# Sixteen value copies for thirty-two, pairs in groups of queries, and probability turns as two turns of 64 rows

## The chip, the cores and the metric

One core of a Trainium2 chip. The metric is device microseconds of one execution, median of three runs: 2372.79 us (2370.24 to 2383.06).

## The reference

A sequence of 512 tokens of width 1024, float32, goes through two layers of a first block and one layer of a second. A layer of the first block is

```
x = x + 0.5 * swiglu(rms_norm(x), ...)            # ffn 1, hidden width 2816
p = rms_norm(x) @ w_in                            # four groups of 256
y = concat(na(p_a), mla(p_b), diff(p_c), gqa(p_d))
x = x + y @ w_out
x = x + 0.5 * swiglu(rms_norm(x), ...)            # ffn 2
x = rms_norm(x)
```

The neighbourhood mixer (na) lays the 512 tokens out as 8 rows of 64 columns. The columns are cut into four blocks of 16; the queries of a block see keys and values of a window of 32 columns in all 8 rows, with a learned bias per relative place and a mask. So a block has 128 queries and 256 keys. The other three mixers are full attention over 512 keys: mla with latents, diff with the difference of two maps and a T5 bias, gqa with two query heads per key head. Each has four heads.

The second block's layer projects x once more and mixes it with forgetting attention (fox, causal, four heads), stick-breaking attention, an RWKV recurrence and a gated linear recurrence.

## The kernel before

All weights are split in a high and a low part and multiplied three times. The feed-forward stages keep TensorE full. The order of work is written out by hand: each engine has one program, and semaphores tie them.

Around the change there are two places.

The attention stage of a layer (lines 1346 to 1443 for TensorE, 2182 to 2228 for ScalarE, 3138 to 3180 for VectorE) works through 40 pairs. A pair (`PAIRS`, line 153) is a mixer, a tile of 128 queries (for na: a block) and two heads or maps. In step s TensorE makes the scores of pair s (line 1391), then turns the probabilities of pair s - 2 (line 1404: blocks of 128x128 against the identity, from SBUF to two PSUM banks), then multiplies the turned probabilities of pair s - 3 with the values (`weigh`, line 1343: two halves of 64 queries on column groups), then does what else is set for the step (turns of queries, keys and mixed values at line 1301; the two latent products at 1311 and 1313). VectorE adds the bias and finds the maxima (3079; 3073 without a bias), makes the difference of the two maps for diff (3064), and takes the mixed values out with the reciprocal of the sum (3104, 3091). ScalarE makes the exponentials (2209) and copies the turned probabilities from PSUM to SBUF (2201; 2199 for diff). For na and diff a turn has four blocks (diff turns only the difference, in one bank), for gqa and mla eight. Scores of na and gqa contract over 64 rows, one head on rows 0 to 63 and the other on 64 to 127, of diff over 32, of mla over 96.

The values of na need another layout than the projection has: for each of the four blocks the 256 tokens of its window, on partitions. `spread_values` (line 970), in SP's queue, makes it with DMAs from SBUF to SBUF: for each token tile t, as soon as ScalarE has copied it out of PSUM with its scale (line 2093, semaphore `proj_copied`), for each block and each of the tile's two grid rows one DMA of 32 tokens by 256 values, 32 in all. All count on one semaphore, `na_v_loaded`; TensorE waits for all 32 ahead of the first product of na. `na_v[0]` holds blocks 0 and 1, `na_v[1]` blocks 2 and 3. The pairs of na are ordered by heads first: blocks 0 to 3 with heads 0 and 1, then blocks 0 to 3 with heads 2 and 3.

The second place is `fox` (line 1560, ScalarE's part at 2402): 8 units of two heads and one query tile, with one to four key tiles each, in the same manner of steps. Its turns stand at line 1589 (with eight blocks at most) and its copies at 2410.

Of the kernel before, what the change touches and what calls it, by code (L numbers as in the profile page):

```python
# [14 lines left out]
P = 128  # L15
# [133 lines left out]
NA_ROOM = 4 * 7 * P  # L149
assert NA_KH == NA_ROWS and NA_B == T and len(NA_FORMS) * HEADS * NA_KEYS <= NA_ROOM  # L150


def attention_pairs():
# [3 lines left out]
    na, mla = ([(m, i, (h, h + 1)) for h in (0, 2) for i in tiles] for m in ("na", "mla"))  # L157
# [189 lines left out]
def build_program(nc, A, out):  # L347
    ctx = ExitStack()
    with ctx:
# [172 lines left out]

        SCORE, TURNED, MIXED, MISC = 0, 2, 4, 6
# [105 lines left out]
        na_v_loaded = sem("na_v_loaded")  # L629
# [129 lines left out]
        small_loaded = sem("small_loaded")  # L759
# [143 lines left out]
        def _(sp):  # L903
# [94 lines left out]
            for n, pieces in enumerate(IN2_PANELS):  # L998
                if n == 2:

                    sp.wait_ge(x_ready, at_layer(DEPTH - 1, 4, 3))
                    sp.dma_start(cols2[:, :], A["cols2"]).then_inc(small_loaded, 16)
                    sp.dma_start(na_flat[:, 0:N_SMALL_CONST], A["small"]).then_inc(small_loaded, 16)
                    sp.dma_start(small("ln_g"), A["rwkv_ln_g_2"][0].partition_broadcast(P)).then_inc(small_loaded, 16)
                    sp.dma_start(small("ln_b"), A["rwkv_ln_b_2"][0].partition_broadcast(P)).then_inc(small_loaded, 16)
                    sp.dma_start(small("lora_w")[0:RW_LORA], A["rwkv_w2_2"][0]).then_inc(small_loaded, 16)
                    sp.dma_start(small("lora_w")[RW_LORA:2 * RW_LORA], A["rwkv_a2_2"][0]).then_inc(small_loaded, 16)
                    for name, w in (("w_a", "lru_w_a_2"), ("w_x", "lru_w_x_2")):
                        for par in range(2):
                            sp.dma_start(small(name)[par * HD:(par + 1) * HD].rearrange("i (h j) -> i h j", h=2),  # L1010
                                         A[w][0, par::2].rearrange("h i j -> i h j")).then_inc(small_loaded, 16)
# [32 lines left out]
        def _(pe):  # L1044
            def turn_x(c):
                pe.wait_ge(x_loaded[c], 16 if c else 16 * 3)
                for k in range(c * KB, (c + 1) * KB):
                    for t in range(T):
                        last = pe.transpose(bank[k][:, t * P:(t + 1) * P], x_tok[:, t, k * P:(k + 1) * P], ident[:, :])
                    last.then_inc(x_turned, 1)  # L1050

# [294 lines left out]
            def attention(l):  # L1346
# [20 lines left out]
                for step in range(N_STEPS):  # L1367
# [25 lines left out]
                    if 0 <= p < N_P:  # L1393
# [71 lines left out]
            def project2():  # L1465
                for m, (n, kind, at, t) in enumerate(IN2_STEPS):
                    if t == 0:
                        split(DEPTH, n)
                    if m == PE_BESIDE["gates"][0]:
                        pe.wait_ge(small_loaded, 16 * 10)  # L1470
# [89 lines left out]
            def fox():  # L1560
                pe.wait_ge(in2_tok, len(IN2_TOK))
                pe.wait_ge(in2_feat, len(IN2_FEAT))
                for step in range(N_FOX + 3):
# [19 lines left out]
                    if 0 <= u < N_FOX:  # L1583
# [3 lines left out]
                        for j in range(2):  # L1587
                            for t in range(FOX_UNITS[u][1] + 1):
                                last = pe.transpose(bank[4 + j][:, t * P:(t + 1) * P],
# [2225 lines left out]
```

## Time and profile before

| | |
|---|---|
| median of 3 runs | 2372.79 us |
| profiled execution | 2371.9 us, span 2370.1 us |
| TensorE matmul busy | 2318.9 us (98%) |
| VectorE busy | 1618.8 us (68%) |
| ScalarE busy | 1144.0 us (48%) |
| mean granted TensorE clock | 0.995 |
| first attention stage | about 475 to 624 us of the span |
| second attention stage | about 1472 to 1620 us |
| fox | about 2186 to 2214 us |

The span is from the first to the last instruction of the profiled execution; the time around it is 1.8 us. Busy shares are averages over stages with different limits, so a stage is read by itself. In the profile PE is TensorE's matmul row, PEld its weight loads, DVE is VectorE, ACT is ScalarE, SP the queue that issues the loads. L1343 is line 1343 of the kernel. A matmul's duration holds its latency, so matmuls of one row overlap.

### The profile page before, as it was taken

Reading aid. Unit: us, or ns where it says so; the run is one execution under the profiler, and the core shown is the slowest. Engines: PE = TensorE matmul, PEld = TensorE weight load, DVE = VectorE, ACT = ScalarE, POOL = GpSimd, SP = SyncE. Lnnn points to the kernel's source line nnn. Section 1 sums busy time; section 2 is a strip of 40 time slices with the busy share of each in tenths; the row PEclk is TensorE's granted clock in tenths of the full one; section 3 lists DMA queues with packets and bytes.
Section 4 is the critical chain, followed back from the end, with each engine's and each line's share of the span. In section 5 each row is a group of like instructions: output and inputs, shape, how many; then the busy total and the mean of one; then the engine's idle time right before and its main releaser. Section 6 shows DMA issues by size and latency. Waiting matters only on the chain.

```text
span 2370.1 us, 40655 instructions
## 1 busy us (share of the span) xinstructions
PE 2318.9 (98%) x16692; PEld 1989.6 (84%) x16692; DVE 1618.8 (68%) x2547; ACT 1144.0 (48%) x1949; POOL 24.0 (1%) x20
## 2 busy tenths in 40 slices
PE   8999999989999999999999999999999999999998
PEld 6999998846789999989999887567899998779687
DVE  7957665558679577689577654686786686682564
ACT  4535444467445354545344445674453455343623
POOL 0000001000000000000000010000000000000000
PEclk9999999999999999999999999999999999999999
DMA  5323342200233334333334422003333333222001
GB/s 155 107 90 102 113 158 91 87 14 18 72 89 100 97 94 115 95 93 104 94 98 117 165 83 80 22 1 90 89 99 98 104 106 118 84 85 72 1 10 65
DMA packets 276649, 205.89 MB, mean 87 GB/s; under 512 B 10673, under 2 KB 263569, under 8 KB 275953
## 3 DMA queue, kind: packets, MB, share of 16 engines
q1 hardware_dynamic: 275632, 195.96, 27.9%
q0 software_dynamic: 832, 7.33, 0.8%
q8 instruction: 133, 2.18, 0.4%
q14 instruction: 52, 0.42, 0.1%
HBM read 199.06 MB, written 2.10 MB: 85 GB/s over the span
## 4 chain that ended last, share of the span: by engine, by line
PE 87%; DVE 6%; ACT 3%; DVEq 2%; issue 1%; DMA 0%; ACTq 0%; SPq 0%
PE bank L1082 23%; PE bank L1174 10%; PE bank L1176 10%; PE bank L1175 10%; PE bank L1151 6%; PE bank L1152 6%; PE bank L1153 6%; PE bank L1360 4%; PE bank L1391 2%; PE bank L1343 2%; PE bank L1454 2%; PE bank L1404 2%; PE bank L1699 1%; PE bank L1301 1%; DVE h_lo L2682 1%
## 5 line engine op out<-in xcount | busy, mean ns | idle before, releaser
L2533 DVE TENSOR_TENSOR w_lo<-raw,w_hi 128x2048 fp32r<-128x2048 f32 (+2 forms) x117 | 240.4, 2055 | 160.0 <-ACT w_hi L1886 159.8
L1886 ACT CAST w_hi<-raw 128x2048 fp32r<-128x2048 f32 (+2 forms) x118 | 202.3, 1715 | 182.3 <-PE bank L1153 90.2
L1151 PE MATMUL bank<-hid_hi,w_hi 128*128 128x512 f32 x704 | 274.7, 390 | 0.9 <-DVE xT L2774 0.9
L1152 PE MATMUL bank<-hid_lo,w_hi 128*128 128x512 f32 x704 | 274.3, 390 | 0.0
L1153 PE MATMUL bank<-hid_hi,w_lo 128*128 128x512 f32 x704 | 273.9, 389 | 0.0
L1174 PE MATMUL bank<-h_hi,w_hi 128*128 128x256 f32 x864 | 245.0, 284 | 2.0 <-DVE w_lo L2718 1.5
L1176 PE MATMUL bank<-h_hi,w_lo 128*128 128x256 f32 x864 | 244.5, 283 | 0.0
L1175 PE MATMUL bank<-h_lo,w_hi 128*128 128x256 f32 x864 | 244.5, 283 | 0.0
L2718 DVE TENSOR_TENSOR w_lo<-raw,w_hi 128x1024 fp32r<-128x1024 f32 x144 | 175.4, 1218 | 3.2 <-ACT w_hi L1958 3.2
L1174 PEld LDWEIGHTS bank<-h_hi,w_hi 128*128 128x128 f32 x864 | 165.7, 192 | 3.9 <-issue 1.6
L1175 PEld LDWEIGHTS bank<-h_lo,w_hi 128*128 128x128 f32 x864 | 165.7, 192 | 0.9
L1176 PEld LDWEIGHTS bank<-h_hi,w_lo 128*128 128x128 f32 x864 | 165.7, 192 | 0.0
L1082 PE MATMUL bank<-h_hi,w_hi 128*128 128x512 f32 x416 | 163.9, 394 | 0.2 <-DVE w_lo L3261 0.2
L1176 PE MATMUL bank<-ops_hi,more_lo 128*128 128x256 f32 x576 | 163.0, 283 | 0.0
L1174 PE MATMUL bank<-ops_hi,more_hi 128*128 128x256 f32 x576 | 162.9, 283 | 0.0
L1082 PE MATMUL bank<-h_lo,w_hi 128*128 128x512 f32 x416 | 162.0, 389 | 0.0
L1082 PE MATMUL bank<-h_hi,w_lo 128*128 128x512 f32 x416 | 161.9, 389 | 0.0
L1082 PE MATMUL bank<-w_hi,h_hi 128*128 128x512 f32 (+2 forms) x448 | 159.8, 357 | 0.0
L1082 PE MATMUL bank<-w_hi,h_lo 128*128 128x512 f32 (+2 forms) x448 | 158.4, 353 | 0.0
L1082 PE MATMUL bank<-w_lo,h_hi 128*128 128x512 f32 (+2 forms) x448 | 158.3, 353 | 0.0
L1151 PEld LDWEIGHTS bank<-hid_hi,w_hi 128*128 128x128 f32 x704 | 132.3, 188 | 28.9 <-issue 2.5
L1153 PEld LDWEIGHTS bank<-hid_hi,w_lo 128*128 128x128 f32 x704 | 132.2, 188 | 27.8
(501 smaller groups left out, 5459.5 us busy)
## 6 DMA issues: line engine op xcount, KB each, us to landing
raw<-in_ffn_w_up SPq DMA_DIRECT2D x88, 512.0 KB, 5.3
raw<-in_ffn_w_gate SPq DMA_DIRECT2D x87, 512.0 KB, 4.0
raw<-in_ffn_w_down SPq DMA_DIRECT2D x96, 384.0 KB, 3.7
raw<-in_w_in SPq DMA_DIRECT2D x60, 512.0 KB, 4.6
raw<-in_w_out SPq DMA_DIRECT2D x24, 512.0 KB, 4.5
raw<-in_ffn_w_down SPq DMA_DIRECT2D x16, 512.0 KB, 4.4
t_bias<-in_t_rel POOLq DMA_DIRECT2D x2, 1792.0 KB, 10.8
raw<-in_w_in SPq DMA_DIRECT2D x8, 416.0 KB, 3.8
```

The lines of the kernel that those rows point to most:

```text
L1082: last = pe.matmul(to, left[a](k), right[b](k), start=(begin and k == 0 and a + b == 0), stop=(end and k == n - 1 and a == 1))
L1151: pe.matmul(to, hi(k), hid_hi[:, k, :], start=(k == 0), stop=False)
L1152: pe.matmul(to, hi(k), hid_lo[:, k, :], start=False, stop=False)
L1153: last = pe.matmul(to, lo(k), hid_hi[:, k, :], start=False, stop=(k == n - 1))
L1174: pe.matmul(columns_at(to), w_hi_[:, k, :], x_hi[:, k, :], start=(begin and k == 0), stop=False, skip_group_check=True)
L1175: pe.matmul(columns_at(to), w_hi_[:, k, :], x_lo[:, k, :], start=False, stop=False, skip_group_check=True)
L1176: last = pe.matmul(columns_at(to), w_lo_[:, k, :], x_hi[:, k, :], start=False, stop=(k == HALF_K - 1), skip_group_check=True)
L1343: last = pe.matmul(to[half * HD:(half + 1) * HD], share[:, half * HD:(half + 1) * HD], value, start=begin, stop=end)
L1360: last = pe.matmul(bank[d % 4], w[:, k, cut], h[:, k, :], start=(begin and k == ks[0] and w is hi and h is h_hi), stop=(end and k == ks[-1 ...
L1886: act.copy(w_hi[:, at, 0:n], raw[:, at, 0:n]).then_inc(hi_ready[at], 1)
L2533: dve.tensor_tensor(w_lo[:, at, 0:n], raw[:, at, 0:n], w_hi[:, at, 0:n].bitcast(F32), ALU.subtract)\
L2718: dve.tensor_tensor(w_lo[:, at, cut], raw[:, at, cut], w_hi[:, at, cut].bitcast(F32), ALU.subtract)\
```

## The change

Values: SP makes 16 DMAs, each of 32 partitions by two token tiles. A copy in the list `NA_COPIES` is a half (token tiles 0 and 1, or 2 and 3) and a block. The half chooses the 64 partitions on which the values go, the grid row the 32 of them. So the keys of a block stand in another order, and the score side follows: ScalarE writes the turned keys of token tile t to place `NA_TILE[t]`, and the host lays the bias out by `NA_KEY_ROWS`. There are two semaphores, one for `na_v[0]` and one for `na_v[1]`; the pairs of na are ordered by blocks first, and TensorE waits for each semaphore ahead of the first product that reads its values. To have a semaphore free, the ten loads of small constants count on `const_loaded` (16 * 12 with the two loads before it) and `small_loaded` goes.

Turns: every turn of probabilities, in the attention stages and in fox, goes through `turn_halves`: each 128x128 block is turned as two turns of 64 rows, rows 0 to 63 into bank b and rows 64 to 127 into bank b + 1, each with 64 columns of result. ScalarE's copy reads the two banks by turns (`from_halves`) and leaves the same turned probabilities as before, in fox packed without gaps.

```
+NA_TILE = [t // 2 + t % 2 * 2 for t in range(T)]
+NA_KEY_ROWS = [2 * NA_TILE.index(n) + r for n in range(T) for r in range(P // GRID_W)]
+NA_COPIES = [(0, 0), (0, 1), (0, 2), (1, 0), (1, 1), (0, 3), (1, 2), (1, 3)]
+N_NA_COPIES = len(NA_COPIES) // 2 * (P // GRID_W)
...
-    na, mla = ([(m, i, (h, h + 1)) for h in (0, 2) for i in tiles] for m in ("na", "mla"))
+    na = [("na", i, (h, h + 1)) for i in tiles for h in (0, 2)]
+    mla = [("mla", i, (h, h + 1)) for h in (0, 2) for i in tiles]
...
+        def from_halves(b, n):
+            return two_banks(b)[:, :, 0:n * HD].rearrange("p h (n q) -> p n h q", n=n)
...
             def spread_values(l):
-                for t in range(T):
-                    sp.wait_ge(proj_copied, at_layer(l, N_COPY, N_COPY - T + t + 1))
-                    for b, a in enumerate(NA_AT):
-                        for r in range(P // GRID_W):
-                            kt, to = divmod((t * (P // GRID_W) + r) * NA_W, P)
-                            sp.dma_start(na_v[b // 2][to:to + NA_W, b % 2 * len(NA_KT) + kt, :],
-                                         proj[r * GRID_W + a:r * GRID_W + a + NA_W, t, NA_V:NA_V + G]).then_inc(na_v_loaded, 16)
+                for half, b in NA_COPIES:
+                    sp.wait_ge(proj_copied, at_layer(l, N_COPY, N_COPY - T + 2 * half + 2))
+                    for r in range(P // GRID_W):
+                        to, a = half * HD + r * NA_W, r * GRID_W + NA_AT[b]
+                        sp.dma_start(na_v[b // 2][to:to + NA_W, b % 2 * len(NA_KT):(b % 2 + 1) * len(NA_KT), :],
+                                     proj[a:a + NA_W, 2 * half:2 * half + 2, NA_V:NA_V + G]).then_inc(na_v_loaded[b // 2], 16)
...
+            def turn_halves(b, parts):
+                for n, part in enumerate(parts):
+                    for half in range(2):
+                        rows_ = slice(half * HD, (half + 1) * HD)
+                        last = pe.transpose(bank[b + half][:, n * HD:(n + 1) * HD], part[rows_], ident[rows_, rows_])
+                return last
...
-                        for j in (1,) if single else (0, 1):
-                            for t in range(key_tiles(p)):
-                                last = pe.transpose(bank[PAIR_TURNED + j][:, t * P:(t + 1) * P],
-                                                    pair_probs(p)[:, j, t * P:(t + 1) * P], ident[:, :])
-                        last.then_inc(probs_turned, 1)
+                        turn_halves(PAIR_TURNED, [pair_probs(p)[:, j, t * P:(t + 1) * P] for j in ((1,) if single else (0, 1))
+                                                  for t in range(key_tiles(p))]).then_inc(probs_turned, 1)
...
-                        if p == FIRST["na"]:
-                            pe.wait_ge(na_v_loaded, at_layer(l, 16 * S // NA_W * NA_B // 2, 16 * S // NA_W * NA_B // 2))
+                        if PAIRS[p][0] == "na" and PAIRS[p][1] % 2 == 0 and PAIRS[p][2][0] == 0:
+                            pe.wait_ge(na_v_loaded[PAIRS[p][1] // 2], at_layer(l, 16 * N_NA_COPIES, 16 * N_NA_COPIES))
...
-                        if PAIRS[p][0] == "diff":
-                            last = act.copy(to, bank[PAIR_TURNED + 1])
-                        else:
-                            last = act.copy(to.rearrange("p (j s) -> p j s", j=2), two_banks(PAIR_TURNED)[:, :, 0:n * P])
+                        to = turned_probs(p)
+                        n = to.shape[1] // P
+                        last = act.copy(to.rearrange("p (n h q) -> p n h q", n=n, h=2), from_halves(PAIR_TURNED, n))
```

Fox's turn and copy are changed in the same way, with `turn_halves(4, ...)` and `from_halves(4, 2 * n // P)`.

## Rows read from the trace of the kernel before

**Rows 1.** The page, the chain that ended last, by engine.

```profile
PE 87%; DVE 6%; ACT 3%; DVEq 2%; issue 1%; DMA 0%; ACTq 0%; SPq 0%
```

**Rows 2.** Timeline of PE, 478 to 516 us: start, length, line, tiles, count [idle before].

```profile
480.14 0.66 PE L1404 MATMUL bank<-ident,spare_hi 128*128 128x128 f32 x4
488.17 1.12 PE L1343 MATMUL bank<-na_v,probsT 128*64 128x64 f32 x16 [7.38 <-issue]
...
492.25 1.12 PE L1343 MATMUL bank<-na_v,spare_lo 128*64 128x64 f32 x16
...
495.01 0.69 PE L1343 MATMUL bank<-na_v,probsT 128*64 128x64 f32 x16
...
497.32 0.69 PE L1343 MATMUL bank<-na_v,spare_lo 128*64 128x64 f32 x16
...
502.32 1.13 PE L1391 MATMUL bank<-work 32*128 32x512 f32 x4
503.38 0.66 PE L1404 MATMUL bank<-ident,probs 128*128 128x128 f32 x4
...
514.19 1.10 PE L1404 MATMUL bank<-ident,probs 128*128 128x128 f32 x8
515.22 0.69 PE L1343 MATMUL bank<-wide,probsT 128*64 128x64 f32 x16
```

**Rows 3.** Timeline of PE in the second layer, 1478 to 1512 us.

```profile
1484.92 1.12 PE L1343 MATMUL bank<-na_v,probsT 128*64 128x64 f32 x16 [7.58 <-issue]
```

**Rows 4.** SP's queue, 462 to 516 us, and the tile na_v: issue to landing.

```profile
466.51 20.27 SPq L977 DMA_DIRECT2D na_v<-wide  x32
...
DMA to landing us min/median/max: 1.8/1.9/2.3
```

**Rows 5.** Busy time by stretch: PE, PEld, DVE, ACT, POOL, then clock, DMA, GB/s.

```profile
482.00:488.00 6.00, 0.00 (x0) 0.00 (x0) 0.00 (x0) 0.58 (x4) 0.00 (x0) 0.59 0.18 49
488.00:494.00 6.00, 5.83 (x48) 4.14 (x50) 1.48 (x7) 2.09 (x7) 0.00 (x0) 0.55 0.01 3
```

**Rows 6.** Timeline of ACT, 462 to 516 us.

```profile
466.38 0.47 ACT L2178 ACTIVATE work<-bank,cols 128x256 f32<-128x256 f32 x1
466.74 0.48 ACT L2179 ACTIVATE work<-bank,cols 128x256 f32<-128x256 f32 x1
...
469.27 0.84 ACT L2093 ACTIVATE wide<-bank,rstd_tok 128x256 f32<-128x256 f32 x2 [1.32 <-PE bank L1082]
...
475.62 0.84 ACT L2093 ACTIVATE wide<-bank,rstd_tok 128x256 f32<-128x256 f32 x2 [1.32 <-PE bank L1082]
```

**Rows 7.** Busy time by stretch of the first attention stage, columns as in rows 5.

```profile
490.00:530.00 40.00, 40.00 (x350) 22.65 (x350) 27.56 (x94) 29.35 (x77) 0.00 (x0) 0.96 0.01 1
530.00:560.00 30.00, 28.46 (x327) 17.86 (x325) 26.70 (x76) 23.69 (x53) 0.00 (x0) 1.00 0.12 37
560.00:590.00 30.00, 28.86 (x311) 18.37 (x312) 23.60 (x68) 22.44 (x53) 0.00 (x0) 1.00 0.01 1
590.00:624.00 34.00, 33.53 (x372) 23.36 (x370) 26.25 (x66) 21.89 (x45) 0.00 (x0) 1.00 0.12 38
```

**Rows 8.** Timeline of PE, 530 to 632 us.

```profile
540.63 1.15 PE L1343 MATMUL bank<-wide,spare_lo 128*64 128x64 f32 x32
...
577.10 1.98 PE L1391 MATMUL bank<-work 96*128 96x512 f32 x4
578.92 1.04 PE L1404 MATMUL bank<-ident,spare_hi 128*128 128x128 f32 x8
```

**Rows 9.** The chain of waits in order of time, turns only: first and last shown.

```profile
491.28 1.04 PE bank L1404 x4
...
616.27 0.87 PE bank L1404 x8
```

**Rows 10.** Timeline of PE in fox, 2186 to 2216 us.

```profile
2198.34 1.04 PE L1589 MATMUL bank<-ident,spare_hi 128*128 128x128 f32 x8
```

**Rows 11.** Groups by line and form, PEld, 466 to 620 us.

```profile
L1391 PEld LDWEIGHTS bank<-work 64*128 64x128 f32 x64 | 5.0, 192 | 6.0 <-ACT probs L2209 2.4 <-issue 1.5 <-ACT spare_hi L2209 0.7
```

More of the change, by code:

```diff
@@ L521, in two_banks, with fox_turned_probs @@
             return banks[:, b * S:(b + 2) * S].rearrange("p (j s) -> p j s", j=2)
+        def from_halves(b, n):
+            return two_banks(b)[:, :, 0:n * HD].rearrange("p h (n q) -> p n h q", n=n)
+        def fox_turned_probs(u, n):
+            return fox_pT[u % 2].rearrange("p j s -> p (j s)")[:, 0:2 * n]
         SCORE, TURNED, MIXED, MISC = 0, 2, 4, 6
@@ L628, in build_program @@
         proj_copied = sem("proj_copied")
-        na_v_loaded = sem("na_v_loaded")
+        na_v_loaded = [sem(f"na_v_loaded{n}") for n in range(NA_B // 2)]
         seg_sq = sem("seg_sq")
@@ L757, in unit_cut @@
             return slice(z * HD, (z + 1) * HD)
-        small_loaded = sem("small_loaded")
         in2_done = sem("in2_done")
@@ L1001, in _ @@
                     sp.wait_ge(x_ready, at_layer(DEPTH - 1, 4, 3))
[L1002 to L1007, printed above, removed]
+                    sp.dma_start(cols2[:, :], A["cols2"]).then_inc(const_loaded, 16)
+                    sp.dma_start(na_flat[:, 0:N_SMALL_CONST], A["small"]).then_inc(const_loaded, 16)
+                    sp.dma_start(small("ln_g"), A["rwkv_ln_g_2"][0].partition_broadcast(P)).then_inc(const_loaded, 16)
+                    sp.dma_start(small("ln_b"), A["rwkv_ln_b_2"][0].partition_broadcast(P)).then_inc(const_loaded, 16)
+                    sp.dma_start(small("lora_w")[0:RW_LORA], A["rwkv_w2_2"][0]).then_inc(const_loaded, 16)
+                    sp.dma_start(small("lora_w")[RW_LORA:2 * RW_LORA], A["rwkv_a2_2"][0]).then_inc(const_loaded, 16)
                     for name, w in (("w_a", "lru_w_a_2"), ("w_x", "lru_w_x_2")):
@@ L1586, in fox @@
                             pe.wait_ge(fox_T, u)
-                        for j in range(2):
-                            for t in range(FOX_UNITS[u][1] + 1):
-                                last = pe.transpose(bank[4 + j][:, t * P:(t + 1) * P],
-                                                    fox_p[u % 3][:, j, t * P:(t + 1) * P], ident[:, :])
-                        last.then_inc(fox_turned, 1)
+                        turn_halves(4, [fox_p[u % 3][:, j, t * P:(t + 1) * P] for j in range(2)
+                                        for t in range(FOX_UNITS[u][1] + 1)]).then_inc(fox_turned, 1)
                     u = step - 3
@@ L1600, in fox @@
                                 o, v = j * P + j * HD, TOK_V + pair * P + j * HD
-                                last = weigh(bank[6][:, o:o + HD], fox_pT[u % 2][:, j, t * P:(t + 1) * P],
+                                share = fox_turned_probs(u, (i + 1) * P)[:, (j * (i + 1) + t) * P:(j * (i + 1) + t + 1) * P]
+                                last = weigh(bank[6][:, o:o + HD], share,
                                              tok2[:, t, v:v + HD], t == 0, t == i)
@@ L2177, in turn_copy @@
                         to = qk_T[:, o:o + 2, :].rearrange("p j (b n) -> p (j b) n", b=NA_B)[:, :, t * w:(t + 1) * w]
+                        cut = slice(NA_TILE[t] * P, (NA_TILE[t] + 1) * P)
                     act.activation(to, q, ACT.Copy, scale=col(kind + "_q_norm"))
@@ L2409, in fox @@
                             act.wait_ge(fox_mix, u - 1)
-                        act.copy(fox_pT[u % 2][:, :, 0:n], two_banks(4)[:, :, 0:n]).then_inc(fox_T, 1)
+                        to = fox_turned_probs(u, n)
+                        act.copy(to.rearrange("p (n h q) -> p n h q", h=2, q=HD), from_halves(4, 2 * n // P)).then_inc(fox_T, 1)
                     u = step
@@ L2498, in rwkv @@
                 split(DEPTH, PAN2_OUT + 1, PAN)
-            act.wait_ge(small_loaded, 16 * 10)
+            act.wait_ge(const_loaded, 16 * 12)
             project2()
@@ L3782, in lay_out @@
     rpb = a["na_rpb"]
-    qr, qc, kr, kc = np.ix_(np.arange(NA_ROWS), np.arange(NA_KW), np.arange(NA_ROWS), np.arange(NA_W))
+    qr, qc, kr, kc = np.ix_(np.arange(NA_ROWS), np.arange(NA_KW), np.array(NA_KEY_ROWS), np.arange(NA_W))
     rel = [rpb[:, :, kr - qr + NA_KH - 1, np.clip(kc - qc - q0 + NA_KW - 1, 0, 2 * NA_KW - 2)] for q0 in NA_FORMS]
```

11 lines of the change are left out of this document (5 added, 6 removed).

## The prediction

> **What bounds the kernel now.** I read the page first, then the chain of waits, then the timeline of each engine around the two attention stages, and the busy time by stretch. The chain is TensorE for 87% of the span [rows 1]: to a first order, what shortens TensorE's own row of work or an idle gap in it shortens the kernel. The largest idle gap is one per layer. At 480.14 us TensorE turns the last probabilities it can, and starts the first neighbourhood product with the values (L1343) only at 488.17 us, after 7.38 us idle [rows 2]; in the second layer it is 7.58 us [rows 3]. The profile says "issue", since it can't name a wait on a copy, so I look at what L1343 waits for there: `na_v_loaded`, all 32 copies of values. SP issues them back to back in 20.27 us, 0.63 us each, from 466.51 to 486.78 us, and one lands 1.9 us after its issue begins [rows 4]: the last at 486.15 + 1.9 = 488.05 us, when TensorE starts. So the gap is SP's issue time. It costs more than itself: the granted clock, 1.00 elsewhere in this stage, means 0.59 over 482 to 488 and 0.55 over 488 to 494 us [rows 5], that is, it fell to its 1.2 GHz level in the gap and stayed there for the first steps behind it.
>
> **Part 1: 16 copies and values in two halves.** The first product now waits for `na_v[0]` alone. Its copies are the first, second, fourth and fifth of the list, and the list is cut by what is projected: (0,0), (0,1), (0,2) wait for token tile 1, whose copy by ScalarE starts at 469.27 and ends at 470.11 us; (1,0) and (1,1) wait for tile 3, ended 476.46 us [rows 6]. Each is two issues. The first six take 6 x 0.63 = 3.8 us, to 473.9 us, and are done before tile 3 is. The next four start at 476.5, the last at 476.5 + 3 x 0.63 = 478.4 us, and land at 480.3 us by 1.9 us. TensorE is at that point at 480.14 + 0.66 = 480.8 us, or some 0.3 us sooner with shorter turns. A copy now carries 64 rows of 1 KB for 32, so I add 0.15 us a layer for a late landing. `na_v[1]` follows with six more issues, the last at 482.1, landed by 484.3 us; its first user is the fifth pair, four steps of some 2.2 us behind 480.8 us, so it is hidden. What goes: 7.38 + 7.58 = 14.96 us, less 0.3.
>
> The cold clock: from the first product to the second it is 492.25 - 488.17 = 4.08 us, and the same step warm is 497.32 - 495.01 = 2.31 us [rows 2]: 1.77 us. The second product takes 1.12 for 0.69 us, 0.43 us more. With no gap I expect no fall, as the clock is back up behind 494 us and the page's row of it shows none of the later, shorter gaps: 2 x 2.2 = 4.4 us. Part 1 in all: 14.7 + 4.4 = 19.1 us.
>
> The new order of the pairs (both head pairs of a block of queries in succession) is needed for this and costs nothing: the same instructions on all engines; VectorE's four sums of squares (0.43 us each) spread over steps 4 to 10 where VectorE is busy 27.56 of 40 us [rows 7]. The renaming of the semaphore for constants has the same loads and waits. SP has 16 issues fewer, and nothing queued behind them is due before 531 us.
>
> **Part 2: every turn in 64-row halves.** A turn of four blocks takes 0.66 us and of eight 1.10 us [rows 2], so a block is 0.11 us and the rest latency. After, there are twice as many instructions, in pairs on row groups 0 to 63 and 64 to 127, each with 64 moving columns for 128. The trace has no such turn. The nearest rows: L1343 works in pairs with 64 moving columns (on column groups), 16 instructions in 0.69 and 32 in 1.15 us [rows 2, 8]: 8 pairs are 0.46 us, 0.058 a pair. And row groups do run side by side: four instructions of 512 columns take 1.13 us on 32-row groups in pairs, 1.98 us when each uses 96 rows and none can pair [rows 2, 8]. So I take 0.058 us a pair: a turn of eight blocks, 8 pairs, 0.69 for 1.10 us, 0.41 less; a turn of four, 4 pairs, 0.69 - 0.23 = 0.46 for 0.66, 0.20 less. Bounds: from below nothing faster than that; from above each half costs what a whole block does, 0.11 us, and a turn of four is 0.44 longer, of eight 0.87 longer.
>
> Changes of shape: where the form of the array changes between two groups, the next group starts 0.07 us before the last one's end (L1391 on 32 rows, ends 503.45; turn at 503.38); where it doesn't (96 rows count as all: ends 579.08, turn at 578.92) it is 0.16 us before [rows 2, 8]. A change costs 0.09 us. Scores of the neighbourhood and gqa pairs use 64-row groups as the new turns do, so 14 changes a layer go; before the 8 turns that follow mla scores one comes.
>
> **A page on this.** The Trainium skill, TensorEngine Tiling (Array Packing), Key Properties, says that a change of tiling mode drains TensorE; the rows agree and put it at 0.09 us, and by either the sum is the same but for the sign at mla's turns.
>
> What of it is on the path. A layer has 8 na, 16 diff (four blocks each), 8 gqa and 8 mla turns (eight each): 24 x 0.20 + 16 x 0.41 = 11.4 us. But the chain of waits holds only 18 turns of four and 8 of eight between 475 and 624 us (the first behind the gap at 491.28, the last at 616.27 us) [rows 9]; the rest stands beside VectorE. By stretch [rows 7]:
> 490 to 530 us: TensorE busy 40.00 of 40, VectorE 27.56, ScalarE 29.35. Nine turns of four and three of eight: 1.8 + 1.2 = 3.0, and eight changes of shape, 0.75: 3.8 us. VectorE and ScalarE have the room.
> 530 to 560: VectorE 26.70 of 30, and its drains fill most of the rest. What TensorE saves here it then waits: 0.2 us.
> 560 to 590: VectorE 23.60 of 30. On the chain stand three turns of four and two of eight, one of them behind mla scores: 0.6 + 0.8 - 0.1 = 1.3 us. Behind 580 us ScalarE and VectorE carry it.
> 590 to 624: three turns of four and one of eight, of which VectorE leaves 0.5, and the turn of eight at 616.27, 0.4: 0.9 us.
> Together 6.2 us a layer, 12.4 us.
> Late next is VectorE (maxima and the difference of the two maps), which is why 11.4 us don't all count.
>
> The eight turns of the last layer (L1589): 40 blocks at 0.051 = 2.0 us, all on the chain (eight blocks 1.04 us [rows 10]). Five more changes of shape than before: 0.45. So 1.6 us.
>
> ScalarE's copy now reads two banks in runs of 64. Copies with 128x256 elements take 0.47 us in runs of 32 (L2178) and 0.48 us unbroken (L2179) [rows 6]: nothing for it; 0 to 0.05 us each is the bound, mostly beside other work.
>
> **Sum.** 19.1 + 12.4 + 1.6 = 33.1 us. The profiled execution took 2371.9 us for a span of 2370.1, so 2338.8 us; the median shown is 0.9 us above it: 2340 us.
>
> **Rivals.** (a) The halves don't pair. A load of 64 rows by 128 columns still takes 192 ns [rows 11]; if a load's time goes by its columns, a half costs the load of a block, and twice the loads one after another eat what the matmuls save. Then only part 1 is left: 2372.8 - 19.1 = 2354 us. Against it: in L1391's pairs the loads were in pairs too, and four of them with their matmuls took 1.13 us. Chance 0.15.
> The Trainium skill, TensorE: Matmul & The Clock Gate, LDWEIGHTS (loading the stationary operand), says that it goes by columns: a 32-row load takes as long as a 128-row one. By that rule alone this case gets part 1 only; the same page, Part 3 (Packing small matmuls), lets loads overlap where the row group differs, which gives my sum.
> (b) VectorE binds sooner: only the first stretch (2 x 3.8) and the last layer (1.6) give: 2372.8 - 19.1 - 9.2 = 2344.5 us. For it: VectorE 26.70 of 30 us. Chance 0.12.
> (c) The bigger copies cost SP twice the issue, 1.27 us. Then the first six end at 477.7, four more start their last at 481.5 and land at 483.6 us: 3 us idle a layer, and as the clock fell within the 7.4 us gap it may fall in this: 2340 + 6 to 10.5, 2348 us. Against it: 0.63 us did not follow bytes in any row. Chance 0.08.
> (d) Slower: row halves of a turn run one after another at a block's price. Per layer 24 x 0.44 + 16 x 0.87 = 24.5 us on TensorE, which then binds throughout, 49 us, and 4.4 us in the last layer; less 19.1, and less the 3.2 us a layer in which TensorE is idle from 530 to 624 us [rows 7]: 2372.8 + 49 + 4.4 - 19.1 - 6.3 = 2401 us. It decides from the point where a block costs 19.1 / 488 = 0.04 us more than before. Chance 0.05, for L1391's pairs speak against it.
> (e) The forecast, 0.60.
>
> **Chances.** Faster by over 0.5% (under 2361 us) in all but (d) and a small rest: 0.92. Within 0.5% (12 us, about what can be told from no change): 0.04, part 1 with halves that cost a little more than blocks. Slower: 0.04. The range: from 2331 us, if three quarters of the 5.8 us a layer that I leave to the other engines (11.4 + 0.6 - 6.2) come too, to 2354 us, case (a).
>
> **What would show it.** Right: no gap over 0.5 us ahead of the first L1343, a clock of 1.00 through the stage; turns of 8 and 16 instructions at 0.46 and 0.69 us, pairs starting together; more VectorE-released waits of TensorE past 530 us. Wrong: a gap left with the last copy's landing at its end (c); turns of 0.66 and 1.10 us (a), or longer (d); or turns as short as I say and a span of the stage that isn't (b).

## The result: 2354.0 us where 2340 was forecast, and scattered

The changed kernel took 2354.0 us, median of 15 runs (2341.35 to 2368.45), beside 2371.12 us for the kernel before (15 runs, 2369.52 to 2383.49). The ratio is 0.9931 [0.9913, 0.9949]: 17.1 us faster, where the sum of the prediction was 33.1 us. The profiled execution is its fastest run: 2341.35 us for a span of 2339.6 us. The spread goes with the mean granted clock of each run:

```
us        clock      us        clock      us        clock
2341.35   0.997      2353.42   0.990      2362.63   0.986
2342.29   0.997      2353.64   0.991      2362.67   0.986
2350.91   0.994      2354.00   0.992      2364.14   0.984
2351.30   0.991      2357.57   0.988      2366.03   0.984
2351.66   0.991      2361.15   0.986      2368.45   0.982
```

The chain that ended last is as before, with one per cent more of VectorE and one less of ScalarE [rows 1]:

```profile
PE 87%; DVE 7%; ACT 2%; DVEq 2%; issue 1%; DMA 0%; SPq 0%; ACTq 0%
```

SyncE's queue for the value copies, and how long one takes to land (to be read beside rows 4):

```profile
468.61 12.69 SPq L986 DMA_DIRECT2D na_v<-wide  x16
DMA to landing us min/median/max: 2.0/2.0/2.9
```

TensorE's timeline (start, length, line, tiles, count [idle before <- what ended it]; to be read beside rows 2 and 10; L1360 was L1343, L1066 was L1404 and L1589):

```profile
479.00 0.69 PE L1360 MATMUL bank<-na_v,probsT 128*64 128x64 f32 x16 [0.28 <-issue]
...
480.63 0.41 PE L1066 MATMUL bank<-ident,late_hi 64*128 64x64 f32 x8
480.97 0.69 PE L1360 MATMUL bank<-na_v,spare_lo 128*64 128x64 f32 x16
...
500.60 0.66 PE L1066 MATMUL bank<-ident,probs 64*128 64x64 f32 x16
...
2169.57 0.71 PE L1066 MATMUL bank<-ident,spare_hi 64*128 64x64 f32 x16
```

The gap of 7.38 us is 0.28 us, the product behind it runs at once in 0.69 us for 1.12, a turn of four blocks takes 0.41 to 0.47 us for 0.66, one of eight 0.66 to 0.72 for 1.10. So far each step is as forecast. What is new stands later in the same stage. Busy time by stretch (PE, PEld, DVE, ACT, POOL, granted clock, DMA, GB/s; rows 7 are those of before):

```profile
490.00:530.00 40.00, 37.62 (x480) 22.67 (x478) 33.75 (x95) 32.41 (x79) 0.00 (x0) 1.00 0.09 28
530.00:560.00 30.00, 27.32 (x380) 16.71 (x378) 26.57 (x80) 24.48 (x57) 0.00 (x0) 1.00 0.01 2
560.00:590.00 30.00, 28.66 (x336) 17.46 (x334) 21.37 (x60) 18.47 (x44) 0.00 (x0) 0.83 0.01 2
...
570.00:574.00 4.00, 2.81 (x48) 1.78 (x50) 3.59 (x7) 2.73 (x7) 0.00 (x0) 1.00 0.02 6
574.00:584.00 10.00, 10.00 (x110) 6.53 (x110) 6.68 (x23) 5.75 (x14) 0.00 (x0) 0.50 0.01 2
```

and TensorE's timeline there:

```profile
521.25 0.69 PE L1360 MATMUL bank<-wide,probsT 128*64 128x64 f32 x16 [0.70 <-DVE spare_hi L3116]
522.65 0.61 PE L1318 MATMUL bank<-ident,wide 128*96 128x128 f32 x4 [0.71 <-DVE wide L2902]
524.95 0.46 PE L1066 MATMUL bank<-ident,spare_hi 64*128 64x64 f32 x8 [0.62 <-DVE spare_hi L3076]
...
573.45 0.46 PE L1066 MATMUL bank<-ident,spare_hi 64*128 64x64 f32 x8 [1.19 <-DVE spare_hi L3076]
573.84 1.88 PE L1360 MATMUL bank<-wide,probsT 128*64 128x64 f32 x32
575.64 2.08 PE L1408 MATMUL bank<-work 32*128 32x512 f32 x4
577.65 1.12 PE L1066 MATMUL bank<-ident,work 64*128 64x64 f32 x16
```

From 490 to 530 us TensorE is now idle for 2.38 us, mostly in three waits close together. Rows 7 have it busy throughout the same 40 us, but that is other work: the stage now runs some 15 us earlier there, and the second and third of the three waits stand in the kernel before as well, behind 530 us:

```profile
537.75 0.62 PE L1301 MATMUL bank<-ident,wide 128*96 128x128 f32 x4 [0.71 <-DVE wide L2890]
...
540.04 0.66 PE L1404 MATMUL bank<-ident,spare_hi 128*128 128x128 f32 x4 [0.62 <-DVE spare_hi L3064]
```

New are the wait of 0.70 us ahead of them, two of 0.87 and 1.02 us behind them, ahead of pairs 20 and 22, and the growth of the wait ahead of pair 31 from 0.93 to 1.19 us. This last one is all of TensorE's idle time from 570 to 574 us. Behind that wait the granted clock is at its 1.2 GHz level for 10 us: the product of 32 instructions takes 1.88 us for 1.15, the turn of eight blocks 1.12 us for 0.66. In the kernel before the clock falls twice, in the two gaps; in this run of the changed one it falls once, and by the mean clocks of the table others have more such time. (Every profile of this document ends with one more fall, which begins after TensorE's last instruction and costs nothing; it is counted nowhere below.)

### The profile page after: what moved, and what is told of

It reads as the page before. It is cut to its first block, busy times and chain, and to the rows that moved or that the text cites. A ratio compares the mean times of both kernels' runs of the same rounds, so it can differ in the third digit from the quotient of the medians.

```text
span 2339.6 us, 41599 instructions
## 1 busy us (share of the span) xinstructions
PE 2292.9 (98%) x17180; PEld 1975.4 (84%) x17180; DVE 1617.7 (69%) x2547; ACT 1140.8 (49%) x1949; POOL 24.0 (1%) x20
## 4 chain that ended last, share of the span: by engine, by line
PE 87%; DVE 7%; ACT 2%; DVEq 2%; issue 1%; DMA 0%; SPq 0%; ACTq 0%
PE bank L1099 23%; PE bank L1191 10%; PE bank L1193 10%; PE bank L1192 10%; PE bank L1168 6%; PE bank L1169 6%; PE bank L1170 6%; PE bank L1377 4%; PE bank L1408 2%; PE bank L1360 2%; PE bank L1468 2%; PE bank L1711 1%; PE bank L1066 1%; PE bank L1318 1%; DVE top L3085 1%
```

## The experiments

The ratio of each is to the kernel before in rounds shared with it. There were three sets of rounds, each on another chip: the four variants of the first subsection, the four kernels of the second, and the four of the third. Times within a set can be compared directly; between sets the kernel before is the only link. Two theories are meant throughout. A: turns that use half of the rows ask too little of the array, so the clock falls. B: TensorE waits for VectorE, for longer since the change made it quicker, and the clock falls behind the waits.

### The two parts by themselves, and two variants of the second

Part 1 alone (turns whole again; ScalarE's copies, fox's turns and the reads of them, which go back to those of before, are left out here):

```diff
-    turn_halves(PAIR_TURNED, [...]).then_inc(probs_turned, 1)
+    for j in (1,) if single else (0, 1):
+        for t in range(key_tiles(p)):
+            last = pe.transpose(bank[PAIR_TURNED + j][...], pair_probs(p)[...], ident[:, :])
+    last.then_inc(probs_turned, 1)
```

> The 16 copies and the order of the pairs alone, every turn whole. By the prediction's first part the gap ahead of the first L1360 is gone: 19 us less than before, 2352 us. Both theories of the clock agree here (whole turns, TensorE never short of work): the clock stays up through the attention stages and the runs lie within 3 us of each other, as most of before do. If instead the copies or the order of the pairs bring the falls of the clock, the runs scatter over 20 us as those of the changed kernel do.

Measured: 2360.06 us (2349.53 to 2365.22, 8 runs), ratio 0.9934 [0.9909, 0.9959]. There are two groups: 2349.5 to 2355.5 us at a mean clock of 0.998 to 1.000, and four runs at 2364.7 to 2365.2 us at 0.991. So the runs within 3 us of each other that both theories expected didn't come. The profile, of a run of the upper group, has two falls. A short one of 3.4 us stands in the first attention stage, behind the two waits that the kernel before has at 537.75 and 540.04 us:

```profile
528.03 0.61 PE L1318 MATMUL bank<-ident,wide 128*96 128x128 f32 x4 [0.71 <-DVE wide L2908]
...
530.32 0.93 PE L1421 MATMUL bank<-ident,spare_hi 128*128 128x128 f32 x4 [0.62 <-DVE spare_hi L3082]
```

```profile
530.50:534.00 3.50, 3.50 (x40) 2.79 (x39) 2.58 (x9) 2.51 (x6) 0.00 (x0) 0.51 0.00 0
```

No turn uses half rows here, so a fall in this stage doesn't need half turns. The other is a fall of 34 us near the end of the kernel. TensorE's timeline ahead of it, then the stretch of the fall:

```profile
2275.63 0.27 PE L1812 MATMUL bank<-mixed,wide 64*64 64x64 f32 x2 [0.58 <-DVE mixed L3691]
...
2277.71 0.38 PE L1812 MATMUL bank<-mixed,wide 64*64 64x64 f32 x5 [0.58 <-DVE mixed L3688]
```

```profile
2275.00:2278.20 3.20, 2.04 (x57) 1.82 (x56) 1.67 (x6) 2.25 (x2) 0.00 (x0) 1.00 0.02 5
2278.20:2312.30 34.10, 34.10 (x295) 24.67 (x290) 12.32 (x34) 11.24 (x57) 0.00 (x0) 0.50 0.10 32
```

Two waits of 0.58 us for VectorE stand ahead of it. They are in every kernel that has no fillers there, since the change doesn't touch this place. Of the kernel before, 12 of 70 runs took 2380.7 to 2383.5 us, at 0.988 or 0.989 where the clock is listed, for 0.995 in most others: I take them for the same fall. (One more run of it, of 11.9 ms, is in no count.)

Part 2 alone (half turns on the kernel before, 32 copies and its gaps kept):

> The 64-row turns alone on the kernel before, 32 copies and their gap kept. By the sums of the prediction 14 us less than before without falls of the clock, 2357 us. Theory A (turns on half rows ask too little of the array and the clock falls at times) and theory B (TensorE finished sooner, waits for VectorE, and the clock falls for the idle time) both say that one or more falls of 10 us come on top, 3.5 us each, so 2357 to 2380 us, scattered. If the runs are as tight as before, the falls need the first part too.

Measured: 2371.47 us (2361.93 to 2390.73, 12 runs), ratio 1.0003 [0.9981, 1.0025], no gain at all in the median, and two runs above the 2380 us that were allowed. The profile has the two falls in the gaps, two more in the attention stages (from 582.6 us for 3.4 us and from 1575.9 us for 20.5 us), both behind the wait of 1.19 us ahead of pair 31, one of 3.4 us in the last layer from 2210.8 us, and the late one of 34 us.

Half turns only where TensorE isn't waiting yet, for pairs 0 to 13 and in the last layer (ScalarE's copies follow the turns; left out here):

```diff
+    if p < 14:
         turn_halves(PAIR_TURNED, [...]).then_inc(probs_turned, 1)
+    else: (the whole turns of above)
```

> The changed kernel with 64-row turns only for the first 14 pairs of a layer (up to about 515 us, where TensorE sets the pace) and in the last layer; whole turns for the other 26 pairs, where VectorE takes most of what they save. Theory A: the stretch of the falls (from 530 us on) has whole turns again, so no falls there: 2341 to 2344 us, tight. Theory B, the same for another reason: TensorE has 0.2 to 0.4 us more work per step there and waits less; 2341 to 2345 us. If falls remain, neither the turns nor their waits behind 515 us are the cause.

Measured: 2343.22 us (2342.42 to 2354.63, 5 runs), ratio 0.9881 [0.9855, 0.9906]; four of five within 2.5 us of each other at 0.998 or 0.999, the fifth at 0.992. Less of the change is faster than the whole of it. The wait ahead of pair 31 is shorter here, as it was before the change:

```profile
576.19 0.66 PE L1425 MATMUL bank<-ident,spare_hi 128*128 128x128 f32 x4 [0.92 <-DVE spare_hi L3090]
```

This fits both theories: fewer half turns (A), and shorter waits (B).

Every half turn made twice:

```diff
-    for n, part in enumerate(parts):
+    for n, part in [x for x in enumerate(parts) for _ in range(2)]:
```

> The changed kernel with every 64-row turn made twice in succession (the same result): TensorE's turns are then about as long as the whole ones (8 pairs for a turn of four blocks 0.69 us against 0.66, 16 pairs 1.15 against 1.10), but all of it on half rows. Time without falls of the clock as with whole turns, 2353 us. Theory A (half rows ask too little of the array): falls remain, 2356 to 2375 us, scattered. Theory B (idle time of TensorE): its waits are those of whole turns, no falls, 2353 to 2356 us, tight.

Measured: 2365.47 us (2356.53 to 2371.28, 11 runs), ratio 0.9963 [0.9944, 0.9981]. Again there are two groups: four runs at 2356.5 to 2358.1 us at 0.998 or 0.999, seven at 2364.5 to 2371.3 us at 0.990 to 0.993. By the times alone this is what theory A said (2356 to 2375 us, scattered), and not the narrow result of B. The profile, of the upper group, says where the time went: it has no fall in the attention stages, where each of the half turns is made twice, a late fall of 30.7 us, and one of 3.4 us in the last layer, behind a wait of 1.22 us for VectorE that the kernel before has too. So far as one profile can, that speaks against A. A turn of four blocks made twice (8 pairs) takes what a turn of eight does:

```profile
480.06 0.66 PE L1066 MATMUL bank<-ident,spare_hi 64*128 64x64 f32 x16
```

### The waits filled, with whole and with half rows

Turns of the identity that nothing reads, put where TensorE would wait (so that the fillers stand between the two waits ahead of a turn, the wait for `probsT_ready` goes first for every pair; it stood second):

```diff
+    def fill(to, n):
+        for _ in range(n):
+            pe.transpose(to[:, 0:P], ident[:, :], ident[:, :])
...
     if p:
         pe.wait_ge(probsT_ready, at_layer(l, N_P, p))
+    fill(bank[PAIR_TURNED], {16: 5, 20: 6, 22: 8, 31: 9}.get(p, 0))
     if single:
         pe.wait_ge(pair_ready, ...)
...
     elif kind == "mla":
+        fill(b, 6 if t == 0 else 0)
```

> The changed kernel, with turns of the identity (128 x 128, into a bank that is overwritten next) put where TensorE waits for VectorE: 5, 6, 8 and 9 of them ahead of the turns of pairs 16, 20, 22 and 31, and 6 ahead of the first turned token tile of the fourth mixer, in both layers; nothing reads them. One is about 0.11 us by the slope of 4 and 8 such turns, so they fill 0.5 to 1.0 us of waits that are 0.62, 0.87, 1.02, 1.19 and 0.71 us long. Theory B (the clock falls behind a wait of TensorE, wherever the row of time in which the chip looks happens to lie): no fall in the attention stages, runs at 2338 us (2341.35 with its one fall of 3.5 us taken off), and some runs 12 us above for the long fall near the end, which is the lottery that the kernel before has too. Theory A (work on half of the rows asks too little): the half turns are all still there, so falls as in the changed kernel, median 2350 to 2356 us.

Measured: 2339.44 us (2338.15 to 2339.72, 5 runs), ratio 0.9857 [0.9833, 0.9881], all at 0.999 or 1.000. The fillers in the timeline, and the third stretch:

```profile
523.05 0.87 PE L1064 MATMUL bank<-ident 128*128 128x128 f32 x6
...
573.44 1.20 PE L1064 MATMUL bank<-ident 128*128 128x128 f32 x9
```

```profile
560.00:590.00 30.00, 28.64 (x365) 17.14 (x363) 24.71 (x66) 20.96 (x50) 0.00 (x0) 1.00 0.01 2
```

With instructions that have no use the kernel is 18 us below the changed kernel in the same rounds (2357.31 us, below), and where the forecast was. Theory A had 2350 to 2356 us. The same with fillers on 64 rows in one row group:

```diff
-        for _ in range(n):
-            pe.transpose(to[:, 0:P], ident[:, :], ident[:, :])
+        for _ in range(2 * n):
+            pe.transpose(to[:, 0:HD], ident[0:HD, :], ident[0:HD, 0:HD])
```

> The same fillers in the same places, each made of two turns of 64 rows in one row group instead of one of 128, so that TensorE is as busy but only half of its rows work. Theory B: the same as with whole fillers, 2338 us with no fall in the attention stages, and some runs 12 us above. Theory A: filling with half rows adds nothing that holds the clock, so the median stays at 2350 to 2356 us whatever the whole fillers do.

Measured: 2351.05 us (2339.44 to 2352.77, 6 runs), ratio 0.9893 [0.9864, 0.9922]. Two runs are at 2339.4 and 2339.8 us, as with whole fillers, and four at 2350.4 to 2352.8 us at 0.991 or 0.992. The median alone is in theory A's range (2350 to 2356 us), so the place of the loss decides. The profile is of one of the four: no fall in the attention stages, and the late one behind the same two waits:

```profile
573.81 1.34 PE L1064 MATMUL bank<-ident 64*128 64x64 f32 x18
...
2261.99 0.27 PE L1814 MATMUL bank<-mixed,wide 64*64 64x64 f32 x2 [0.58 <-DVE mixed L3692]
...
2264.06 0.38 PE L1814 MATMUL bank<-mixed,wide 64*64 64x64 f32 x5 [0.58 <-DVE mixed L3689]
```

```profile
2264.80:2298.90 34.10, 34.10 (x289) 24.69 (x289) 12.48 (x34) 11.24 (x57) 0.00 (x0) 0.50 0.09 32
```

A fall of that length accounts for the 12 us between the groups. So in the attention stages half rows hold the clock as well as whole ones, and theory A isn't what explains the falls there. Fillers near the end too:

```diff
+    fill(bank[RW_SA], {1: 4, 2: 4}.get(g, 0))
     pe.wait_ge(state_ready, g)
```

> The kernel with whole fillers, and four more turns of the identity ahead of each of the two state products near the end where TensorE waits 0.59 and 0.58 us for VectorE, just ahead of the place where the long fall of the clock began in two other profiles. Theory B: this fall goes as well, and all runs lie within 3 us of 2338 us. Theory A (the 20 us of products of 64 x 64 ahead of that place ask too little, not the waits): some runs in three stay 12 us above.

Measured: 2339.43 us (2337.82 to 2339.99, 6 runs), ratio 0.9856 [0.9832, 0.9880]. All narrow, but so were the five with nothing filled there. The changed kernel as it is, in the same rounds:

> The changed kernel as it is, on the same chip in the same rounds, for comparison and for a second profile of it. Both theories: runs scattered from 2341 to 2368 us. Theory B: each fall in the profile starts right behind a stretch in which TensorE waited for over 1.1 us in sum, and the candidates are those of the first profile's waits: 519 to 525, 570 to 576, 1504 to 1510 and 1555 to 1560 us, and near 2264 us. Theory A: falls start inside the stretches of half turns without a wait ahead of them.

Measured: 2357.31 us (2343.95 to 2366.35, 10 runs), ratio 0.9931 [0.9905, 0.9957], the same as the first time. Its profile, of a run at 2360.42 us, has three falls. TensorE's timeline ahead of each:

```profile
573.15 0.46 PE L1066 MATMUL bank<-ident,spare_hi 64*128 64x64 f32 x8 [1.20 <-DVE spare_hi L3076]
...
1511.77 0.69 PE L1360 MATMUL bank<-wide,probsT 128*64 128x64 f32 x16 [0.70 <-DVE spare_hi L3116]
1513.16 0.61 PE L1318 MATMUL bank<-ident,wide 128*96 128x128 f32 x4 [0.71 <-DVE wide L2902]
1515.46 0.60 PE L1066 MATMUL bank<-ident,spare_hi 64*128 64x64 f32 x8 [0.62 <-DVE spare_hi L3076]
...
2272.73 0.38 PE L1807 MATMUL bank<-mixed,wide 64*64 64x64 f32 x5 [0.58 <-DVE mixed L3682]
```

and the falls by stretch:

```profile
573.50:597.40 23.90, 23.90 (x175) 13.37 (x172) 13.43 (x36) 11.64 (x26) 0.00 (x0) 0.50 0.00 1
597.40:601.00 3.60, 3.60 (x38) 1.81 (x36) 2.55 (x6) 2.67 (x6) 0.00 (x0) 1.00 0.00 0
1512.00:1515.60 3.60, 2.27 (x28) 1.15 (x25) 3.30 (x10) 2.38 (x7) 0.00 (x0) 1.00 0.02 8
1515.60:1519.00 3.40, 3.40 (x46) 2.79 (x44) 2.77 (x10) 2.54 (x7) 0.00 (x0) 0.50 0.02 5
...
2273.40:2307.50 34.10, 34.10 (x290) 24.68 (x290) 12.39 (x34) 11.24 (x57) 0.00 (x0) 0.50 0.10 32
```

Each begins within 1 us of the end of a wait at one of the places named beforehand (later by what the falls ahead of it cost). Whether a fall comes varies from run to run: the wait near 573 us is there in both profiles of this kernel, with a fall of 10 us in the one and 24 us in the other, and the waits near 1513 us had a fall in the second only. In this run 61 us pass at half clock, and the run is 21 us above the filled kernel: one microsecond of it costs 0.34 us, an estimate from this pair of runs.

### One wait back, and the late fall by itself

The filled kernel less one filler, the nine turns ahead of pair 31:

```diff
-    fill(bank[PAIR_TURNED], {16: 5, 20: 6, 22: 8, 31: 9}.get(p, 0))
+    fill(bank[PAIR_TURNED], {16: 5, 20: 6, 22: 8}.get(p, 0))
```

> The kernel with all whole fillers, the two near the end too, less one of them: the nine turns of the identity ahead of pair 31, so that the wait of 1.19 us there, once a layer, is open again. Theory B: falls come back behind this wait and nowhere else, in some runs in one layer and in some in both: times from 2339.5 us (no fall) to about 2347 us (two falls of 10 us at 3.5 us each), up to 2355 us where a fall is longer. Theory A (half rows): the half turns are the same as in the filled kernel, so all runs stay at 2338 to 2340 us.

Measured: 2342.99 us (2337.72 to 2357.40, 6 runs), ratio 0.9886 [0.9860, 0.9912]. Three runs are at 2337.7 to 2340.7 us, as with all fillers, and three at 2345.3, 2352.3 and 2357.4 us at 0.996, 0.993 and 0.990. Time at the lower clock comes back with this one wait, as B has it, and more than I allowed (2357 for 2355 us at the most). Under theory A all runs would have stayed at 2338 to 2340 us. The changed order of the two waits for a turn is still in this kernel, so it is the fillers that hold the clock, and not that order. The profile is of one of the first three, so that the falls of the others stand behind this wait isn't seen, only that they come with it; its own one fall, of 3.4 us, is at 2099.9 us, in another stage. The wait itself:

```profile
574.70 0.46 PE L1071 MATMUL bank<-ident,spare_hi 64*128 64x64 f32 x8 [1.28 <-DVE spare_hi L3084]
```

The kernel with fillers on 64 rows, with the same near the end:

```diff
     fill(bank[PAIR_TURNED], {16: 5, 20: 6, 22: 8, 31: 9}.get(p, 0))
...
+    fill(bank[RW_SA], {1: 4, 2: 4}.get(g, 0))
```

> The kernel with fillers on 64 rows, with the same fillers on 64 rows near the end too, at the two state products where TensorE waits 0.59 and 0.58 us. Without the two, four of six runs were 12 us above the others, with a fall of 34 us from just behind these waits. Theory B: none of the runs is, all lie at 2338 to 2341 us. Theory A (the stretch of 64 x 64 products ahead of the place asks too little): as before, half of the runs or more at 2351 us.

Measured: 2339.28 us (2338.34 to 2340.51, 4 runs), ratio 0.9861 [0.9844, 0.9877]. The late waits are gone:

```profile
2260.12 0.71 PE L1064 MATMUL bank<-ident 64*128 64x64 f32 x8
...
2262.20 0.71 PE L1064 MATMUL bank<-ident 64*128 64x64 f32 x8
```

The kernel before with the two late fillers and nothing else:

> The kernel before with the four turns of the identity ahead of each of the two state products near the end, and nothing else. Theory B: its runs at 2380 to 2383 us go, and all lie at 2369 to 2372 us; the two falls behind the gap for the values stay. Theory A: two or three runs in ten stay at 2381 us.

Measured: 2371.26 us (2369.16 to 2375.21, 12 runs), ratio 0.9996 [0.9988, 1.0005]. None of 12 runs is at 2381 us, and one, at 2375.2 us, is above what was expected. By the 12 in 70 of the kernel before, two at 2381 us were to be expected, and none would come one time in ten. But in this set of rounds the kernel before had only one such run in 17, and by that none in 12 comes one time in two: this run shows little.

Part 1 alone with the two late fillers:

> The kernel with 16 copies and all turns whole, with the same two fillers near the end. Of its eight runs without them four were at 2364.7 us, with a fall of 34 us near the end, and the rest at 2349.5 to 2355.5 us. Theory B: all runs at 2349 to 2355 us, which gives part 1 by itself as 15 to 21 us; its one wait spot in the attention stages near 527 us still gives a short fall now and then. Theory A: half of the runs stay at 2364.7 us.

Measured: 2352.76 us (2351.81 to 2355.46, 6 runs), ratio 0.9918 [0.9903, 0.9933]. Without them, in the first set, half of the runs were at 2364.7 us or above. The profile has two falls of 3.4 us, one at 1517.8 us behind the same two waits as in part 1 alone, and one at 2101.5 us, which is shown below. Taken together, and going by the time and clock of each run, the late fall came in 16 of 35 runs of the variants that have the late waits and no other long falls (part 1 alone 4 of 8, half turns twice 7 of 11, early half turns 1 of 5, whole fillers 0 of 5, half fillers 4 of 6), and in none of 28 runs with late fillers (6, 4, 12 and 6). That points to the late waits as the cause, and it isn't clean: 22 of the 28 were run in the third set, where even the kernel before, which has the waits, had such a time in 1 of 17 runs. Within the second set it is 4 of 11 against 0 of 6, which chance alone gives about one time in seven. Products of 64 x 64 that ask too little would be expected to keep the fall: they are all still there.

**All 14 profiles together** have 22 falls (those behind TensorE's last instruction left out). Six begin inside the gaps of 7.4 to 8.1 us ahead of the first product with the values. Fourteen begin within about 0.8 us of the end of a wait of TensorE for VectorE, which lasted 0.58 to 1.22 us. Two have no wait of over 0.4 us just ahead. Whether a fall came behind a wait went with its length, but not with that alone. At the places that bear on the argument:

```
place                                     length, us     falls behind it
ahead of pair 31, half turns              1.18 to 1.28   4 of 8
ahead of pair 31, whole turns             0.92 to 0.93   0 of 10
two waits near 522 us (540 before)        0.71 + 0.62    3 of 18
two late waits                            0.58 + 0.58    5 of 9
last layer, behind fox                    1.21 to 1.22   2 of 14
last layer, some 40 us later              1.23           0 of 14
```

The wait ahead of pair 31 is the clearest: at the length that it had before the change no profile has a fall there, at the length that the change gave it half have one. With half turns but less of a wait there (fillers in four profiles, turns made twice in one) it is 0 of 10.

## Why the prediction was right and where it failed

**The gap (part 1): right.** The bound of SyncE's queue was read rightly: 16 copies, and a wait of 0.28 us. Issues cost 12.69 us for 16, the wait of SyncE for the later token tiles included, and landing 2.0 us for 1.9; rival (c) is out. Part 1 by itself is 2371.26 - 2352.76 = 18.5 us, both with the late fillers and in the same set of rounds, for 19.1 forecast. The same subtraction without the fillers gives 11 us, and the worth of the part would have been misjudged by the share of late falls that 8 runs happened to have.

**The half turns: right in price.** 0.41 to 0.47 us for a turn of four blocks (0.46 forecast), 0.66 to 0.72 for one of eight (0.69), 0.71 in the last layer for 1.04; the two halves of a block start 0.007 us apart, and the next block 0.06 us later. Rivals (a) and (d) are out. That the median came to rival (a)'s 2354 us is a coincidence: its mechanism isn't there. The Trainium skill, TensorE: Matmul & The Clock Gate, LDWEIGHTS (loading the stationary operand), would by itself have had loads eat the saving; the trace goes with Part 3 (Packing small matmuls) of the same page.

**What of it counts on the path: right within 1 us, once the clock is held.** With all waits filled (on 64 rows) the kernel is 2352.76 - 2339.28 = 13.5 us below part 1 alone with late fillers, in the same rounds, for 12.4 + 1.6 = 14.0 us forecast. Part 1 alone has short falls in its profile there, which cost some 2 us by the 0.34 us above, so the turns are worth a little less than that. Kept for the early pairs and the last layer only, the best runs are at 2342.4 to 2343.2 us against 2337.8 to 2340.0 of the filled kernel in another set, so the later half turns give some 3 to 4 us for both layers, where I had 2 x (0.2 + 1.3 + 0.9) = 4.8 behind 530 us, and some more between 515 and 530 us. Rival (b), 2344.5 us, is near that variant and not the kernel. The whole sum, 2340 us, is what the filled kernels take (2339.3 to 2339.4).

**"With no gap I expect no fall": wrong, and this is the step that failed.** The sum has no term for it, and none of the rivals (a) to (e) is it. I took the clock to fall in idle gaps of several microseconds only, because the page's row of it showed none of the shorter ones of the kernel before. That row has slices of 59 us (2370.1 / 40), and the longest wait for VectorE in the attention stages was 0.93 us, this one of the kernel before:

```profile
589.68 0.66 PE L1404 MATMUL bank<-ident,spare_hi 128*128 128x128 f32 x4 [0.93 <-DVE spare_hi L3064]
```

The change itself made it 1.19 us, opened two of 0.87 and 1.02 us and put one of 0.70 us ahead of the two near 522 us that were there already. Behind it the granted clock is 0.83 over 560 to 590 us, where my sign of being right was 1.00 through the stage. I had written that TensorE would wait for VectorE past 530 us, and had counted that wait as saving nothing; it can cost, 0.34 us for each microsecond that the clock then stays at half. With the fillers as the measure, the falls cost 2354.0 - 2339.4 = 14.6 us (17.9 us within the second set), nearly all of the difference between forecast and result, and they undo part 2: the changed kernel has the ratio to the kernel before that part 1 alone has, 0.9931 and 0.9934. Not all of this is the change's doing. The late fall costs some 12 us where it comes, and its waits are in the kernel before too; how the 14.6 us divide between it and the falls in the attention stages isn't known, since only two of the changed kernel's runs were profiled.

The range held the time only at its edge. It allowed for other prices of the steps and not for falls of the clock that make the runs of one kernel differ by 27 us; the 12 of 70 runs of the kernel before at 2381 us, one of which stands among its three times, was the sign of it that I passed over.

The Trainium skill, TensorE: Matmul & The Clock Gate, HAM oscillation — how this bites in real kernels, speaks of long idle gaps, and I reasoned as it does. The section behind it, A second HAM failure mode: psum-queue depth-cycling, says that frequent short idles between groups of matmuls make the clock swing too. The rows above go with the second in that short idles are enough, and beyond it in that they needn't be frequent: one wait of 1.19 us, or two of 0.58 us, stood ahead of a fall.

**What stays open.** Waits alone don't decide. None of the 14 profiles has a fall behind this wait of the changed kernel, which all have at its place with 1.45 to 1.50 us, among products of 128 rows:

```profile
1075.08 0.35 PE L1191 MATMUL bank<-h_hi,w_hi 128*128 128x256 f32 x1 [1.46 <-DVE w_lo L2730]
```

And two short falls had no such wait ahead, one in part 1 alone with late fillers and one in the filled kernel less one filler: the clock fell behind a product on four rows. TensorE's timeline and the stretches of the first:

```profile
2098.70 1.98 PE L1557 MATMUL bank<-mixed,ident 4*128 4x512 f32 x4
2100.61 0.50 PE L1104 MATMUL bank<-h_hi,w_hi 128*128 128x512 f32 x1
...
2102.16 0.63 PE L1104 MATMUL bank<-h_hi,w_lo 128*128 128x512 f32 x1
```

```profile
2097.00:2101.50 4.50, 4.50 (x16) 2.56 (x15) 4.27 (x5) 0.00 (x0) 0.00 (x0) 1.00 0.00 0
2101.50:2104.90 3.40, 3.40 (x10) 2.63 (x9) 3.26 (x5) 0.00 (x0) 0.00 (x0) 0.50 0.91 285
```

So something of theory A may hold for work on very few rows; no run here separates it. Nor is it known why one fall lasts 3.4 us and another 24 or 34 us, or what makes the late fall come in 4 of 6 runs of one variant and in 12 of 70 of the kernel before. That the late waits bring it is likely by the count and not shown within one set of rounds.

## What to carry to other kernels

When a change makes TensorE quicker than the engine that feeds it, price the new waits as possible falls of the clock and not as zero: here about half of the forecast gain went that way, and it came back by useless turns in the waits, or in good part by leaving TensorE slower where it would wait. Read the mean granted clock of every run beside its time before comparing variants, and compare runs at the same clock: a median over runs in two groups measures how often the clock fell. Where the times of a kernel have one outlier that a lower clock explains, look for its place before putting a range on a change.

## What the runs showed of the hardware

- Behind waits of 0.6 to 1.2 us TensorE's granted clock fell to 1.2 GHz for 3.4 to 34 us, in some executions of one program and not in others; with the waits in the attention stages filled no profile has a fall there. The time lost was 0.34 us for each microsecond at half clock in the run where it can be counted.
- Turns that nobody reads, 0.7 to 1.3 us of them in each wait, held the clock, on half of the rows as on all: 2339.28 us (64 rows) and 2339.43 us (128 rows), with fillers near the end in both.
- Turns of 64 rows in two row groups go in pairs that start 0.007 us apart: four pairs take 0.41 us and eight 0.66 us, 0.06 us a pair for 0.11 us a block of 128 x 128.
